# The down bias moved between experts 15 and 16, and expert weights loaded as 2 MB pieces of four neighbouring rows per partition

## What is computed

```python
logits = h @ w_router + b_router
top_val, top_idx = top_k(logits, 4);  gates = softmax(top_val)
# for each expert e and the rows xe of h that chose it, in blocks of 64 rows
gt = minimum(xe @ w_gate[e] + b_gate[e], LIMIT)
up = clip(xe @ w_up[e] + b_up[e], -LIMIT, LIMIT)
y  = ((up + 1) * gt * sigmoid(ALPHA * gt)) @ w_down[e] + b_down[e]
# x += sum over the chosen experts of gate * y, then a last normalisation
```

## Time and profile before

| what | value |
|---|---|
| time, median of 3 runs | 1299.94 us (1296.65 to 1300.36) |
| the profiled execution's own time | 1296.7 us |
| its span, first to last instruction | 1294.4 us |
| TensorE busy | 1230.3 us (95%) |
| VectorE busy | 471.9 us (36%) |
| ScalarE busy | 187.5 us (14%) |
| data moved | 428.58 MB, mean 331 GB/s |
| share of the chain that ended last | PE 62%, DMA 14% |

### The profile page before, as it was taken

How to read it: one execution, slowest core, us unless ns; L and a number is a source line. 1 busy time by engine, 2 the same in 40 slices (tenths; PEclk the granted TensorE clock), 3 DMA queues, 4 the chain that set the end, 5 groups by cost and what they waited for, 6 DMA issues and landing times.

```text
span 1294.4 us, 20525 instructions
## 1 busy us (share of the span) xinstructions
PE 1230.3 (95%) x8084; PEld 561.0 (43%) x8084; DVE 471.9 (36%) x1031; ACT 187.5 (14%) x369; POOL 59.9 (5%) x103
## 2 busy tenths in 40 slices
PE   7999899998999999999999999999999999999995
PEld 5676689865323333333333333333333333333331
DVE  5748752333153223323233223323233223332324
ACT  2362224123101001001001001001001001000101
POOL 0204250010000000000000000000000000000000
PEclk9999899999979999999999999999999999999998
DMA  9320300374949999999999999999999999999994
GB/s 263 109 74 36 138 4 4 81 286 151 389 169 407 423 422 422 422 421 422 422 423 422 422 422 423 422 422 422 421 422 423 422 421 422 422 422 423 422 421 163
DMA packets 82000, 428.58 MB, mean 331 GB/s; under 512 B 16287, under 2 KB 30031, under 8 KB 32798
## 3 DMA queue, kind: packets, MB, share of 16 engines
q1 hardware_dynamic: 80522, 427.80, 81.7%
q10 hardware_dynamic: 1436, 0.16, 0.1%
HBM read 424.80 MB, written 3.11 MB: 331 GB/s over the span
## 4 chain that ended last, share of the span: by engine, by line
PE 62%; DMA 14%; ACT 1%; DVE 1%; issue 1%; SPq 1%; DVEq 0%
PE bank L1669 42%; DMA arena<-in_w_up_dram 14%; PE bank L1715 6%; PE bank L1649 5%; PE bank L1656 3%; PE bank L1607 1%; PE bank L1554 1%; ACT arena L1515 1%; PE bank L1677 1%; PE bank L1718 1%; SPq L1346 1%; PE bank L1612 0%; DVE arena L1948 0%; PE bank L1544 0%; DVE arena L1940 0%
## 5 line engine op out<-in xcount | busy, mean ns | idle before, releaser
L1669 PE MATMUL bank<-ring,arena 128*64 128x512 f32 x2048 | 457.9, 600 | 18.7 <-ACT arena L1515 17.8
L1669 PEld LDWEIGHTS bank<-ring,arena 128*64 128x64 f32 x2048 | 145.0, 138 | 307.3 <-issue 306.8
L1669 PE MATMUL bank<-arena 128*64 128x512 f32 x1024 | 226.9, 592 | 3.1 <-DMA arena<-in_w_up_dram 3.1
L1669 PEld LDWEIGHTS bank<-arena 128*64 128x64 f32 x1024 | 72.6, 136 | 146.1 <-issue 129.9
L1928 DVE TENSOR_TENSOR arena<-arena,bank 128x512 f32<-128x512 f32 (+1 forms) x192 | 118.0, 680 | 33.7 <-PE bank L1718 18.0
L511 PE MATMUL bank<-arena,ring 128*128 128x336 f32 x352 | 103.5, 452 | 1.1 <-DVE arena L645 1.1
L1715 PE MATMUL bank<-arena 64*128 64x512 f32 (+1 forms) x384 | 99.0, 616 | 3.7 <-ACT arena L1522 0.6
L1649 PE MATMUL bank<-arena 128*64 128x512 f32 (+1 forms) x396 | 90.8, 592 | 1.1 <-DVE arena L1809 1.1
L1855 DVE TENSOR_SCALAR arena<-arena 96x64 bf16<-96x64 f32 x33 | 8.3, 250 | 217.5 <-PE bank L1669 217.5
L511 PEld LDWEIGHTS bank<-arena,ring 128*128 128x128 f32 x352 | 67.0, 192 | 34.7 <-issue 3.1
L1916 DVE TENSOR_SCALAR arena<-bank 128x512 f32<-128x512 f32 x32 | 22.1, 692 | 160.9 <-PE bank L1677 160.9
(11 more groups left out here) (351 smaller groups left out, 849.8 us busy)
## 6 DMA issues: line engine op xcount, KB each, us to landing
ring<-in_w_gate_dram SPq DMA_DIRECT2D x128, 1024.0 KB, 16.9
arena<-in_w_up_dram SPq DMA_DIRECT2D x128, 1024.0 KB, 19.9
ring<-in_w_down_dram SPq DMA_DIRECT2D x128, 1024.0 KB, 18.5
ring<-in_w_in_dram SPq DMA_DIRECT2D x11, 1024.0 KB, 5.2
ring<-in_w_out_dram SPq DMA_DIRECT2D x4, 1024.0 KB, 8.6
arena<-in_x_prompt_dram SPq DMA_DIRECT2D x2, 512.0 KB, 5.1
out_wkv_sample_dram<-arena SPq DMA_DIRECT2D x4, 256.0 KB
arena<-in_x_prompt_dram SPq DMA_DIRECT2D x2, 448.0 KB, 4.3
```

The lines of the kernel that those rows point to most:

```text
L1669: mm = M.matmul(bank[64 * hb:64 * hb + 64, b, :], tokens(cc), w[:, c, 512 * hb:512 * hb + 512], start=(cc == 0), stop=(w3 == 2 and cc == K ...
```

## The change

It has two independent halves and some bookkeeping.

1. The down bias leaves expert 0. The loop over experts is cut in two, 1 to 15 and 16 to 31 (`HALF` is 16), and between the two TensorE runs `down_bias`: three transposes, a wait for ScalarE's copy, and six matmuls with 32 rows, each into a bank that VectorE has emptied (`cmb_read`), each with its own addition on VectorE. TensorE waits at the end until all six were added (`bd_read`).
2. A unit is 2 MB: rows 4p to 4p + 3 of half a matrix, 16384 contiguous bytes per partition. An expert has six units (`EU`), in six slots of 2 MB. `product` waits twice per matrix instead of four times, and `turn` reads every fourth column of its source, a step of 16 bytes.
3. The output projection's units move to slots 4 to 7 of `ring`, and the recurrence's `Kx` and `Bx` to slot 3. `gffn` comes in two small transfers instead of four.

```diff
-            return IN_SLOTS[t % 4] if t < UNITS_IN else 3 + t - UNITS_IN
+            return IN_SLOTS[t % 4] if t < UNITS_IN else 4 + t - UNITS_IN
...
-        EXT_SLOTS = 4
-        EU = 12
-        landed = unit_landed + [lsem(f"ext_landed{i}") for i in range(EXT_SLOTS)]
-        SLOT = [7, 0, 1, 2, 8, 9, 10, 11, 3, 4, 5, 6]
+        BIG = 2 * UNIT
+        EU = 6
+        HALF = NE // 2
+        landed = [lsem(f"big_landed{i}") for i in range(EU)]
+        BIG_SLOT = [0, 1, 4, 5, 2, 3]
+        FREED_BY = [0, 0, 0, 0, UNITS_IN + 2, UNITS_IN + 4]
...
-            w = a[("w_gate", "w_up", "w_down")[n // 4]][0][bass.ds(e, 1)]
-            u = n % 4
-            return w.rearrange("o (u p q) n -> u p (o q) n", u=4, q=2)[u]
+            w = a[("w_gate", "w_up", "w_down")[n // 2]][0][bass.ds(e, 1)]
+            return w.rearrange("o (u p q) n -> u p (o q) n", u=2, q=4)[n % 2]
...
                     for m in range(4):
                         mm = M.transpose(bank[:, 4, m * P:m * P + P],
-                                         src.rearrange("t (u p q) -> t u q p", u=2, q=2)[:, m // 2, m % 2, :], ident)
+                                         src.rearrange("t (p q) -> t q p", q=4)[:, m, :], ident)
...
-                    for u in range(4):
+                    for u in range(2):
                         wait_expert_unit(pe, it, first + u)
                         w = unit_tile(first + u)
-                        for c in range(2):
-                            cc = 2 * u + c
+                        for c in range(4):
+                            cc = 4 * u + c
...
+                def down_bias():
+
+                    for i, (t0, m) in enumerate(TILES):
+                        mm = M.transpose(bank[0:NE, 5, t0:t0 + m], gates[0:m, i, :], ident[0:m, 0:m])
+                    mm.then_inc(F["gt_turned"], 1)
+                    pe.wait_ge(F["bdown_in"], 16)
+                    pe.wait_ge(F["gt_ready"], 1)
+                    for i, (t0, m) in enumerate(TILES):
+                        for hb in range(2):
+                            k = 2 * i + hb
+                            pe.wait_ge(F["cmb_read"], HALF * 6 + k + 1)
+                            M.matmul(bank[0:m, CMB_BANKS[k], :], gT32[0:NE, t0:t0 + m],
+                                     bdown[0:NE, 512 * hb:512 * hb + 512], start=True, stop=True).then_inc(F["bd_done"], 1)
+                    pe.wait_ge(F["bd_read"], 6)
...
-                with pe.Fori(1, NE) as it:
+                with pe.Fori(1, HALF) as it:
+                    body(it)
+                down_bias()
+                with pe.Fori(HALF, NE) as it:
                     body(it)
...
+                for i, (t0, m) in enumerate(TILES):
+                    for hb in range(2):
+                        k = 2 * i + hb
+                        dve.wait_ge(F["bd_done"], k + 1)
+                        o = acc[0:m, i, 512 * hb:512 * hb + 512]
+                        V.tensor_tensor(o, o, bank[0:m, CMB_BANKS[k], :], ALU.add).then_inc(F["bd_read"], 1)
```

More of the change, by code:

```diff
@@ L184, in wait_unit @@
         def wait_unit(eng, t):
-            eng.wait_ge(unit_landed[slot_no(t)], 16 * (t // 4 + 1) if t < UNITS_IN else 16)
+            earlier = sum(1 for k in range(t) if slot_no(k) == slot_no(t))
+            eng.wait_ge(unit_landed[slot_no(t)], 16 * earlier + 16)
         def chain(eng, s):
@@ L1508, in _, with body @@
                         .then_inc(F["h_ready"], 1)
-                def body(n, first=False):
+                def body(n):
                     act.wait_ge(F["t1_ready"], n + 1)
@@ L1519, in body @@
                     A.copy(ys, bank[:, 2, :]).then_inc(F["ys_ready"], 1)
[L1520 to L1525, removed]
+                body(0)
+                with act.Fori(1, HALF) as it:
+                    body(it)
+                act.wait_ge(F["gt_turned"], 1)
+                A.copy(gT32[0:NE, :], bank[0:NE, 5, 0:NT]).then_inc(F["gt_ready"], 1)
+                with act.Fori(HALF, NE) as it:
                     body(it)
@@ L1685, in body @@
                     pe.wait_ge(F["cmb_read"], n * 6 + 2)
[L1686 removed]
+                    product(n, 2, 1, lambda cc: xT[:, cc % 4, cc // 4, :], 1).then_inc(F["u_done"], 1)
                     if first:
@@ L1699, in body @@
                     pe.wait_ge(F["cmb_read"], n * 6 + 6)
-                    product(n, 8, 2, lambda cc: aT[:, cc % 4, cc // 4, :], 2)
+                    product(n, 4, 2, lambda cc: aT[:, cc % 4, cc // 4, :], 2)
                     pe.wait_ge(F["xg_ready"], n + 2)
                     turn(xg).then_inc(F["x_done"], 1)
[L1703 to L1706, removed]
                     pe.wait_ge(F["pgt_ready"], n + 1)
                     pe.wait_ge(F["ys_ready"], n + 1)
-                    if first:
-                        pe.wait_ge(F["bdown_in"], 16)
-                        pe.wait_ge(F["gt_ready"], 1)
                     for i, (t0, m) in enumerate(TILES):
@@ L1714, in body @@
                             o = bank[0:m, CMB_BANKS[2 * i + hb], :]
[L1715 to L1720, removed]
+                            M.matmul(o, PgT[64 * hb:64 * hb + 64, i, 0:m], ys[64 * hb:64 * hb + 64, :],
+                                     start=True, stop=True).then_inc(F["cmb_done"], 1)
+                def down_bias():
[11 more added lines that the diff above has]
+                    pe.wait_ge(F["bd_read"], 6)
                 pe.wait_ge(F["p_ready"], 1)
@@ L1932, in _ @@
                 make_table()
-                with dve.Fori(1, NE) as it:
+                with dve.Fori(1, HALF) as it:
+                    body(it)
+                for i, (t0, m) in enumerate(TILES):
[4 more added lines that the diff above has]
+                        V.tensor_tensor(o, o, bank[0:m, CMB_BANKS[k], :], ALU.add).then_inc(F["bd_read"], 1)
+                with dve.Fori(HALF, NE) as it:
                     body(it)
```

33 lines of the change are left out of this document (15 added, 18 removed).

## The result

| kernel | median us | runs | ratio to before, 95% interval |
|---|---|---|---|
| before, shared by the same chip | 1300.15 (1296.65 to 1302.60) | 4 | |
| changed | 1287.26 (1281.95 to 1288.99) | 4 | 0.9896 [0.9858, 0.9934] |

The change makes the kernel about 13 us faster. I had forecast 1313 us, slower. The profiled execution took 1281.95 us with a span of 1280.0; the other three had spans of 1284.4 to 1287.0 and mean granted clocks of 0.981 to 0.982 against its 0.987. The traces are compared by spans, the kernels by medians. Much of what executions differ by arises early: the turn at the end of expert 0 stands at 346.37 in this profile and at 349.10 in that of the same kernel in experiment 3. So I also give, for each profile, the stretch from expert 0's turn to the last combine: 930.7 us before (346.88 to 1277.60), 916.9 after (346.37 to 1263.22).

What follows compares the result with a forecast made beforehand. TensorE was taken to bound the kernel until the slots' lead is used up, the transfers after it. From 1299.9 us, - 26.7 + 13.6 + 26.0 = +12.9 gave 1313 us, range 1282 to 1322.

Steps and rivals of the forecast that it cites:

- Part 3: Transposes in `turn`: the 16-byte source step adds 100 ns to each, 26.0 us in all, bounds 0 and 34.8.
- the sign: Whole kernel: slower by 12.9 us, given 62%; it would turn to faster below 50 ns per transpose.
- the step of 16 bytes is hidden: Rival for the transposes in `turn`: the step costs under 30 ns each, giving 1287 us; chance 28%.
- Part 1: Expert 0 without the bias saves 21.9 us, and the end wait for transfers goes, 4.8 us: gain 26.7 us.
- Part 2: Bias block between experts 15 and 16, with nothing beside it on TensorE: costs 13.6 us, bounds 8.0 and 16.4.
- The wait: End of the bias block: TensorE waits for VectorE's last addition, with the hand-over back 0.85 us.
- the slow product: Product right behind the bias block: it starts at the lowered clock and takes 2.7 us longer.
- Part 4: Slots and 2 MB pieces: larger pieces gain or lose nothing unless transfers get slower, 0 us.

Runs made afterwards that it cites:

- experiment 3: The changed kernel run once more, unaltered, on the chip of the two halves: 1286.76 us, ratio 0.9896.
- experiment 7: Changed kernel with the six bias matmuls on 128 rows instead of 32, the added rows zeros: 1285.30 us, ratio 0.9886.
- experiment 1: Kernel before with only the down bias moved between experts 15 and 16, still 1 MB units and 8-byte step: 1288.12 us, ratio 0.9898.
- experiment 4: Changed kernel plus five groups of 16 transposes with source steps of 1 to 16 float32 before the output projection: 1295.46 us, one execution.
- experiment 2: Kernel before with only the 2 MB units and 16-byte step, bias left in expert 0: 1294.15 us, ratio 0.9950.
- experiment 6: Changed kernel with gate transposes before expert 15's combine, no block wait for the additions, VectorE's table after the bias: 1282.29 us, ratio 0.9868.
- experiment 8: Changed kernel with the separate bias block right after expert 0 and VectorE's table after the bias additions: 1285.99 us, ratio 0.9897.
- experiment 9: Kernel before, bias still inside expert 0's combine, its six bias matmuls on 128 rows with zeros: 1287.73 us, ratio 0.9902.
- experiment 10: Changed kernel with the edits of experiment 6 and experiment 7 together: 1279.53 us, ratio 0.9831.

## Why the prediction was wrong

**Part 3 failed, and with it the sign.** This is the step of the prediction that was wrong: the term of 26.0 us for the step of 16 bytes, which measured under 1 us. I priced it at 100 ns per transpose because the step from contiguous to 8 bytes had lengthened the load record by 67 ns. The error was twofold. I extended a trend from two points, and I took a longer load for a later matmul. The load went to 209 ns, and the steps of 32 and 64 bytes have 192 and 196. The spacing of the transposes, which is what costs time, moved from 0.117 to (0.75 - 0.388) / 3 = 0.121, some 0.9 us in the kernel; the period's 0.025 us more per expert, 0.8 in all, agrees. The rival "the step of 16 bytes is hidden" holds, with its 1287.

The Trainium skill, "SBUF — State Buffer", "Door 1: The DMA port swizzle", gave me cover for that price with its 16-byte lines. The cover was thin. A load at half the contiguous pace would take 280 ns and cost +73, not the +100 that I wrote, and the same note goes on to name "4 fp32" as what one can stride for free, which I passed over. No run here shows such a cost for TensorE's loads: not at a step of four float32 nor at sixteen.

**Part 1 held.** Expert 0 lost 21.9 us less the new 1.9, and no transfer is waited for at the end. What I hadn't seen is that the long combine covered VectorE's table. I had asked what is late once that stall goes, and looked only among the transfers.

**Part 2 was the right mechanism with a size off:** 10.3 instead of 13.6. The matmuls took 5.69 in place of 3.06 + 5.91, since a bias matmul between its own kind takes 0.90 us (5.40 / 6, experiment 7) and the 1.02 of expert 0 is that of one between matmuls on other rows; and the clock fell only near the end of the six (0.65 over 794 to 798). In expert 0 of before it had fallen 2.7 us after the combine began, not 3.1: a mean of 0.90 over 348 to 352 puts the fall at 351.2. The wait was 1.14, not 0.85, the slow product 2.45, not 2.7. Of the other blocks of 32-row matmuls at that place, experiment 3 came to 10.3 us and experiments 1 and 4 to 12.0, so when the clock falls and returns moves this term by some 2 us between executions.

What went with the fall was the number of rows: with 32 the clock fell at the bias in every profile (before, the changed kernel, experiments 1, 2, 3, 4, 6 and 8), with 128 in none (7, 9 and 10). Experiments 6 and 10, and before and experiment 9, differ in nothing else. Why rows matter isn't shown by any run, nor is where between 32 and 128 it turns, nor whether the added rows may hold anything but zeros. Gaps don't decide it: experiment 6 has none and lost the clock, experiment 10 has none and kept it, and experiment 7 pauses 0.72 and 1.18 us and kept it. The Trainium skill, "TensorE: Matmul & The Clock Gate", Part 1, puts the drop down to idle gaps; these traces disagree with it here, as that of before did.

**Part 4 held.** The pieces are worth nothing that the runs can tell once the bias is out of the way (1286.76 against 1288.12), though they run at 429 instead of 422 GB/s. They were worth 6 us only in a kernel whose transfers had lost their lead.

The near agreement of the median, 1287.26, with the rival's 1287 owes something to chance: the block was 3.3 us cheaper than in the sum, the table 1.9 and the period 0.8 dearer, and the rest is within the spread of executions.

## What to carry to other kernels

When a stretch of matmuls reads twice its usual time with TensorE busy, look at the granted clock before anything else, and if the matmuls there use few rows, try them on 128 with zeros: that one edit was worth as much here as moving the work out (1287.73 and 1288.12). A longer record of a load that is hidden behind a matmul was no price here (209 ns against 140, with 0.12 us between matmuls against 0.11); measure the spacing, and build a series of sizes before extending a trend from two. When a stall is taken away, list what every other engine did under it, too. And before two profiles are compared by their spans, see how much of the difference lies before the place that was changed: here it was up to 8.4 us.

## What the runs showed of the hardware

- At the six float32 matmuls on 32 rows TensorE's clock fell from 2.4 to 1.2 GHz in all eight profiles that have them, with the engine busy throughout in experiment 6; the same on 128 rows left it up in all three. The fall cost the product behind them 1.4 to 2.9 us as well (8.46 to 10.03 against 7.09).
- A transpose whose source has a step of 2, 4, 8 or 16 float32 costs the same: loads of 207, 212, 192 and 196 ns, and matmuls 0.12, 0.12, 0.11 and 0.11 us apart. With a contiguous source the load is 140 ns and the matmuls 0.11 us apart.
- A bias matmul of 512 columns at the full clock takes 0.90 us among its own kind and 1.04 (12.5 / 12) where it alternates with the combine's. The ordinary combine's, which alternate between two halves of the rows, take 2.85 / 6 = 0.48, and the product's, which alternate between two halves of the output partitions, 7.09 / 16 = 0.44.
- Weight transfers in pieces of 16384 contiguous bytes per partition ran at 429 GB/s, of 8192 bytes at 422 (experiments 1 and 9 too).
